# Down projections of three dense feed forwards split into single passes, with one rounding moved ahead of DMA issues

## The reference

```python
mod = cond @ w_ada[layer] + b_ada[layer]                 # 6 x 1024 numbers per layer
def swiglu(x, w1, w3, w2): return (silu(x @ w1) * (x @ w3)) @ w2          # first0
def conv_ffn(h, w_up, conv_w, conv_b, w_down):                            # even, odd
    gate, val = split(h @ w_up)
    gate = causal_dwconv(gate, conv_w) + conv_b          # 3 taps along the tokens
    return (silu(gate) * val) @ w_down
```

## Time and profile before

| | us |
|---|---|
| median of 3 runs | 2593.45 (2589.7 to 2593.66) |
| the profiled execution, its own time | 2587.25 |
| its span | 2585.4 |
| PE busy | 2504.0 |
| DVE busy | 1773.6 |
| ACT busy | 1199.2 |
| POOL busy | 333.2 |

### The profile page before, as it was taken

How to read it: one execution, slowest core, us unless ns; L and a number is a source line. 1 busy time by engine, 2 the same in 40 slices (tenths; PEclk the granted TensorE clock), 3 DMA queues, 4 the chain that set the end, 5 groups by cost and what they waited for, 6 DMA issues and landing times.

```text
span 2585.4 us, 36960 instructions
## 1 busy us (share of the span) xinstructions
PE 2504.0 (97%) x14304; PEld 2173.7 (84%) x14304; DVE 1773.6 (69%) x1949; ACT 1199.2 (46%) x1273; POOL 333.2 (13%) x97
## 2 busy tenths in 40 slices
PE   5999999999999999999999999899999999999999
PEld 4889998878888888888888888788999889988998
DVE  5832775768888888888888888365289777863122
ACT  3213213117676767676767676322322446653221
POOL 0005541000000000000000000010454100001542
PEclk8989999999999999999999999999999999999999
DMA  9745884767989998999999989230678443332442
GB/s 367 308 162 211 345 321 171 293 244 266 351 333 350 334 348 335 347 335 346 336 346 337 345 338 361 82 130 1 222 310 320 170 144 144 131 131 103 175 168 92
DMA packets 90383, 656.18 MB, mean 254 GB/s; under 512 B 10032, under 2 KB 10288, under 8 KB 10800
## 3 DMA queue, kind: packets, MB, share of 16 engines
q1 hardware_dynamic: 80928, 589.34, 60.8%
q10 hardware_dynamic: 9360, 65.52, 6.3%
HBM read 653.76 MB, written 1.05 MB: 253 GB/s over the span
## 4 chain that ended last, share of the span: by engine, by line
PE 71%; issue 17%; POOL 6%; DVE 3%; ACT 2%; ACTq 0%; DMA 0%; POOLq 0%; DVEq 0%; SPq 0%
PE bank L1158 70%; POOL ring_rounded L732 6%; PE bank L1703 1%; DVE work L1856 1%; DVE rstd L1904 0%; ACT ff_mid L1060 0%; DVE xT L1850 0%; DMA ring<-stream_dram 0%; DVE ring L1856 0%; DVE ring_rounded L1844 0%; ACT ff_silu L1059 0%; ACT work_rounded L773 0%; DVE yT L1850 0%; ACTq L753 0%; POOL work L692 0%
## 5 line engine op out<-in xcount | busy, mean ns | idle before, releaser
L1844 DVE TENSOR_TENSOR ring_rounded<-ring,work_rounded 128x2048 fp32r<-128x2048 f32 x372 | 842.1, 2289 | 143.6 <-ACT work_rounded L907 122.0
L1158 PE MATMUL bank<-work_rounded,proj_rounded 128*128 128x512 f32 x1792 | 614.3, 406 | 0.7 <-DVE proj_rounded L1844 0.3
L907 ACT ACTIVATE work_rounded<-ring 128x2048 fp32r<-128x2048 f32 x224 | 428.4, 1913 | 0.0
L1158 PEld LDWEIGHTS bank<-work_rounded,proj_rounded 128*128 128x128 f32 x1792 | 338.1, 189 | 77.1 <-issue 2.9
L1158 PE MATMUL bank<-ring_rounded,proj_rounded 128*128 128x512 f32 x896 | 354.1, 395 | 0.0
L1158 PE MATMUL bank<-work_rounded,ff_hid_rounded 128*128 128x512 f32 x896 | 302.5, 398 | 1.8 <-DVE ff_hid_rounded L1844 1.8
L1158 PE MATMUL bank<-yT_rounded,ring_rounded 128*128 128x256 f32 x960 | 271.6, 283 | 0.0
L1158 PE MATMUL bank<-hT,ring 128*128 128x256 f32 x1088 | 247.4, 388 | 1.1 <-ACT hT L797 1.1
L1158 PEld LDWEIGHTS bank<-hT,ring 128*128 128x128 f32 x1088 | 211.0, 195 | 37.8 <-issue 8.5
L1158 PE MATMUL bank<-ff_hid,ring 128*128 128x256 f32 x1056 | 232.9, 379 | 0.0
L1158 PEld LDWEIGHTS bank<-ff_hid,ring 128*128 128x128 f32 x1056 | 198.4, 190 | 25.9
(11 more groups left out here) (286 smaller groups left out, 4294.9 us busy)
## 6 DMA issues: line engine op xcount, KB each, us to landing
ring<-stream_dram SPq DMA_DIRECT2D x561, 1024.0 KB, 4.8
work<-stream_dram ACTq DMA_DIRECT2D x56, 1024.0 KB, 9.3
params<-params_dram ACTq DMA_DIRECT2D x1, 1728.5 KB, 28.8
consts<-consts_dram ACTq DMA_DIRECT2D x1, 1568.0 KB, 37.4
cond<-cond_dram ACTq DMA_DIRECT2D x2, 512.0 KB, 4.0
xT<-x_dram ACTq DMA_DIRECT2D x1, 1024.0 KB, 10.3
out_dram<-xT SPq DMA_DIRECT2D x1, 1024.0 KB, 3.9
consts<-consts_dram ACTq DMA_DIRECT2D x1, 577.0 KB, 32.2
```

Source lines behind the costliest of these rows:

```text
L907: act.activation(up_high[u][half], ring[:, (moe_first + s + half) % RING, :], ACT.Copy)\
L1158: return pe.matmul(o, lhsT=a, rhs=b, start=start, stop=stop, skip_group_check=True)
L1844: return dve.tensor_tensor(o, a, b, op)
```

## The change

The down slots of chunks 0 to 9 are made into single passes as the up slots are; the down of chunk 10 stays a float32 product. ACT rounds the down slot (`high(c, odd, 2)`) after `high(c, odd, 1)`, and before it the two hidden tiles of the chunk in one 128 x 512 instruction into `ff_hid_high` (`hid_high`); DVE subtracts that to get `ff_hid_low` (`leave_low`, `hid_low`), after the first two of the six dots where there are dots; POOL subtracts a third slot per chunk. `down(c)` waits on `split_low` and `hid_low` and does 48 float32r matmuls. ACT does `high(c, odd, 0)` ahead of `load_modulation`. Two more buffers of a slot lie in `work`, the tiles in `h_heads`; `cond` moves in memory.

```diff
+        ff_down_high = [work_r[:, mod_at + (MOD_GROUP + u) * SLOT:mod_at + (MOD_GROUP + 1 + u) * SLOT] for u in range(2)]
...
-        SPLITS = 2 * (DENSE_CHUNKS - 1)
-        PAIR_SPLITS = 4
+        SPLITS = 3 * (DENSE_CHUNKS - 1)
+        HID_SPLITS = DENSE_CHUNKS - 1
+        PAIR_SPLITS = 6
+        split_buffers = [w_high[0], w_high[1], ff_down_high[0], w_high[2], w_high[3], ff_down_high[1]]
...
+                    pool.wait_ge(weights_used, place[f"in{n}"])
+                    pool.wait_ge(split_low, dense_before[n] * SPLITS)
...
-                    at = (first + r // 2 * 3 + r % 2) % RING
+                    at = (first + r) % RING
                     pool.wait_ge(split_high, q + (before + 1))
-                    pool.tensor_tensor(ring_r[:, at, :], ring[:, at, :], f32(w_high[r]), ALU.subtract)\
+                    pool.tensor_tensor(ring_r[:, at, :], ring[:, at, :], f32(high), ALU.subtract)\
...
+                    if not final:
+                        high(c, odd, 0)
                     if n + 1 < len(plan) and not isinstance(c, int):
                         load_modulation(n + 1, c - 2)
-                    if not final:
-                        high(c, odd, 0)
                     if isinstance(c, int) and c == 0:
                         high(c, odd, 1)
                     tiles(c, odd)
                     if not (isinstance(c, int) and c == 0) and not final:
                         high(c, odd, 1)
+                    if not final:
+                        act.wait_ge(ffn_hid, base + 2 * c + 2)
+                        if not isinstance(c, int) or c >= 2:
+                            act.wait_ge(weights_used, c * 3 + (first - 1))
+                        act.activation(ff_hid_high[:, 2 * odd:2 * odd + 2, :], ff_hid[:, 2 * odd:2 * odd + 2, :], ACT.Copy)\
+                           .then_inc(hid_high, 1)
+                        high(c, odd, 2)
...
+                    else:
+                        r = 3 * c + 2
+                        q = splits + r + 1
+                        pe.wait_ge(split_low, q if i is None else i * PAIR_SPLITS + q)
+                        parts = [p.rearrange("p (j n) -> p j n", j=2)
+                                 for p in (ff_down_high[c % 2], ring_r[:, (first + 2 + r) % RING, :])]
+                        t = dense_before[n] * HID_SPLITS + c + 1
+                        pe.wait_ge(hid_low, t if i is None else i * 2 + t)
...
+                                last = mm3(o, [p[:, j, d * P:d * P + P] for p in parts],
+                                           (ff_hid_high[:, b, :], ff_hid_low[:, b, :]),
+                                           i is None and c == 0 and j == 0 and d % 2 == 0, False)
...
+                    def leave_low():
+                        dve.wait_ge(hid_high, c + (dense_before[n] * HID_SPLITS + 1))
+                        tt(ff_hid_low[:, 2 * odd:2 * odd + 2, :], ff_hid[:, 2 * odd:2 * odd + 2, :],
+                           f32(ff_hid_high[:, 2 * odd:2 * odd + 2, :]), ALU.subtract).then_inc(hid_low, 1)
+
...
+                            dve.wait_ge(hid_low, c + (dense_before[n] * HID_SPLITS - 1))
...
-                        mod_parts(n + 1, c - 2, range(MOD_GROUP))
+                        mod_parts(n + 1, c - 2, range(1))
+                        leave_low()
+                        mod_parts(n + 1, c - 2, range(1, MOD_GROUP))
+                    elif not (isinstance(c, int) and c == DENSE_CHUNKS - 1):
+                        leave_low()
```

More of the change, by code:

```diff
@@ L200, in build_program @@
         work = sb("work", shapes["work"])
-        cond = sb("cond", [P, D])
         ring_r, yT_r, ff_hid_r, work_r = (rounded[name] for name in ("ring", "yT", "ff_hid", "work"))
@@ L206, in build_program @@
         h_heads = sb("h_heads", shapes["h_heads"])
+        cond = sb("cond", [P, D])
         xT = sb("xT", [P, KD, T])
@@ L366, in build_program @@
         h_low = pflat_r[:, SLOT:2 * SLOT].rearrange("p (k t) -> p k t", k=KD)
-        assert mod_at >= 2 * SLOT
+        ff_down_high = [work_r[:, mod_at + (MOD_GROUP + u) * SLOT:mod_at + (MOD_GROUP + 1 + u) * SLOT] for u in range(2)]
+        assert mod_at >= 2 * SLOT and mod_at + (MOD_GROUP + 2) * SLOT <= work_n - D
+        ff_hid_high, ff_hid_low = (rounded["h_heads"][:, a * 4 * T:(a + 1) * 4 * T].rearrange("p (b t) -> p b t", b=4)
+                                   for a in range(2))
         weights_here = [sem(f"weights_here{i}") for i in range(RING)]
@@ L393, in build_program @@
         split_low = sem("split_low")
+        hid_high, hid_low = sem("hid_high"), sem("hid_low")
         ffn_mid = sem("ffn_mid")
@@ L726, in feed_forward, with low @@
                     .then_inc(*low_pool.step("h"))
-                def low(r, q):
-                    at = (first + r // 2 * 3 + r % 2) % RING
+                def low(r, q, high):
+                    at = (first + r) % RING
                     pool.wait_ge(split_high, q + (before + 1))
-                    pool.tensor_tensor(ring_r[:, at, :], ring[:, at, :], f32(w_high[r]), ALU.subtract)\
+                    pool.tensor_tensor(ring_r[:, at, :], ring[:, at, :], f32(high), ALU.subtract)\
                         .then_inc(split_low, 1)
@@ L736, in feed_forward @@
                     for r in range(PAIR_SPLITS):
-                        low(r, i * PAIR_SPLITS + r)
+                        low(r, i * PAIR_SPLITS + r, split_buffers[r])
             for n, kind in enumerate(plan):
@@ L1094, in high @@
                         act.wait_ge(weights_used, c * 3 + (first + w - 3))
-                    act.activation(w_high[2 * odd + w], ring[:, (first + at) % RING, :], ACT.Copy)\
+                    act.activation(split_buffers[3 * odd + w], ring[:, (first + at) % RING, :], ACT.Copy)\
                        .then_inc(split_high, 1)
@@ L1750, in split_here @@
                 def split_here(c, w, i):
-                    q = splits + 2 * (c - 1) + w + 1
+                    r = 3 * (c - 1) + w
+                    q = splits + r + 1
                     pe.wait_ge(split_low, q if i is None else i * PAIR_SPLITS + q)
-                    return w_high[2 * ((c - 1) % 2) + w], ring_r[:, (first + 3 * c - 1 + w) % RING, :]
+                    return split_buffers[r % PAIR_SPLITS], ring_r[:, (first + 2 + r) % RING, :]
                 def mm3(o, w, x, start, stop):
@@ L1790, in down @@
                 def down(c, i=None, final=False):
[L1791 to L1795, removed]
+                    if final:
+                        at = ff_down(first, c, chunks)
+                        arrive(at)
+                        pe.wait_ge(ffn_hid, base + 2 * c + 2)
+                    else:
+                        r = 3 * c + 2
+                        q = splits + r + 1
+                        pe.wait_ge(split_low, q if i is None else i * PAIR_SPLITS + q)
[3 more added lines that the diff above has]
+                        pe.wait_ge(hid_low, t if i is None else i * 2 + t)
                     for j in range(2):
@@ L1798, in down @@
                         for d in range(KD):
-                            last = mm(bank(d // 2, d % 2 * T, d % 2 * T + T), w2[:, j, d * P:d * P + P],
-                                      ff_hid[:, b, :], i is None and c == 0 and j == 0 and d % 2 == 0,
-                                      final and j == 1)
+                            o = bank(d // 2, d % 2 * T, d % 2 * T + T)
+                            if final:
+                                last = mm(o, down_k(at)[:, j, d * P:d * P + P], ff_hid[:, b, :], False, j == 1)
+                            else:
+                                last = mm3(o, [p[:, j, d * P:d * P + P] for p in parts],
+                                           (ff_hid_high[:, b, :], ff_hid_low[:, b, :]),
+                                           i is None and c == 0 and j == 0 and d % 2 == 0, False)
                             if final and j == 1 and d in (1, 3, 5):
```

## The result

The changed kernel takes 2654.83 us (median of 4 runs, 2653.57 to 2656.31) against 2591.57 of the kernel before in the same comparison (median of 4, 2582.69 to 2593.66). The ratio is 1.0256, with a 95% interval of [1.0244, 1.0269]. The profiled execution took 2654.68 us, 1.8 more than its span.

What follows compares the result with a forecast made beforehand. In `first0` and `even` a ring of ACT, DVE and POOL was taken to bound, in `odd` PE. `first0` +38.7, `even` +49.0 and `odd` -9.6 gave +78.1, on the median 2593.45 a forecast of 2671 us, range 2615 to 2690.

Steps and rivals of the forecast that it cites:

- The exclusion of DVE and POOL: In chunks with dots: while POOL subtracts no dot proceeds, exactly one does between two subtractions; chance of this mechanism 74%.
- Rivals 1: Rival 1: third subtraction costs nothing, intervals stay near 19.5 us, kernel faster at 2582, or 2565 with head overlapped; chance 5%.
- Rival 2: No head, as POOL does next chunk's w = 0 in it; 21.2 us bounds, +23.5 in all, 2617; chance 11%.
- Head: Stretch from a chunk's last dot to POOL's start, the shared resource idle: in `first0` 3.73 us before, 4.26 after, +0.53.
- +1.6: Growth of the head in `even`, where the convolution stands in it too; taken between +1.4 and +2.2 us.
- Moving the rounding buys nothing: ACT's new order: w = 0 leaves the head but w = 1 stands behind issues and SiLUs, so no gain.
- Third subtraction: POOL's added subtraction takes 4.55 us of the shared resource in each chunk; bounds 4.55 and 0.
- Hidden tiles: DVE's 128 x 512 subtraction adds 0.65 us to each chunk's ring, or 0 if it shared nothing with POOL.
- Intervals of 25.3 and 26.3: Predicted us between modulation issues per chunk in `first0` and `even`, +5.7 and +6.8, six intervals each.
- The tail: From group 7's issue to the last matmul, 33.0 us before: 28.7 in `first0` (-4.3), 32.4 in `even` (-0.6).
- the down in `odd`: Single passes take 5.76 us instead of 6.72, 0.96 less on PE for each of 10 chunks: -9.6.
- rival 3: PE's clock falls throughout, so its 17.3 us per chunk becomes 34.6 and bounds: 2790; chance 5%.

Runs made afterwards that it cites:

- all_dve: The changed kernel with all three subtractions of a chunk on DVE in place of POOL: 2548.18 us, ratio 0.9845 to the kernel before.
- order_only: The kernel before with only ACT's new order (first slot's rounding ahead of the modulation issues), no single-pass downs: 2602.08 us, ratio 1.006 to the kernel before.
- issue_first: The changed kernel with ACT's old order, modulation issues ahead of the rounding of w = 0: 2647.22 us, ratio 1.0232 to the kernel before.
- low_first: The changed kernel with DVE's 128 x 512 subtraction ahead of all six dots instead of after two: 2661.26 us, ratio 1.0293 to the kernel before.

## Why the prediction was right

**What bounds.** The exclusion of DVE and POOL held in every kernel in which POOL subtracts. With POOL out, no dot of the feed forwards takes longer than 1.15 us (all_dve); with all three subtractions on it, all three alternate with DVE's work. The chain of waits read over 264 to 410 us of the changed kernel has no PE in it, and 30% for the landing of the modulation group. That landing isn't the bound: it falls under POOL's first subtraction, and all_dve has the same transfers at 17.43 us a chunk.

**Rivals 1 and 2** fell. The third subtraction isn't free: POOL's idle time ahead of a set is 9.40 us, as it was the earlier trace rows, and is dots and head. Rival 2, the head of 4.26 gone and the interval 21.2, didn't come: no run with three subtractions on POOL is under 24.5.

**Head.** Predicted 4.26, measured 4.26, and 4.27 in order_only. In `even` +1.6 was a choice between 1.4 and 2.2: POOL starts 5.28 us after the last dot (2034.20 to 2039.48), +1.55, and order_only's interval there is +1.46. "Moving the rounding buys nothing" was right: it costs, as the two terms say, 13.7 us by itself, and issue_first gets 6 of it back.

**Third subtraction, +4.55.** POOL's three take 15.64 us, against 10.09 for two: 4.55 and one more gap of 1.0, in which a dot lies that had stood behind the set.

**Hidden tiles, +0.65.** 350.72 to 355.61 on DVE is one POOL subtraction waited out and 0.5 to 0.6 of its own; alone it takes 0.6. The Trainium skill (SBUF — State Buffer, Who interferes with whom) gives the rule that makes this a term, and the trace agrees: 4.97 us beside POOL, 0.68 with POOL silent. No run leaves this subtraction out alone, so its size is read from the one chunk.

**Sizes.** Intervals of 25.3 and 26.3 were 25.09 and 25.91. The hidden tiles account for most of the difference in `first0`: they add 0.47 us after POOL's last (355.14 to 355.61), for 0.65. In `even` the head has its 1.55, and from POOL's start to the last dot's end it is 20.60 us (2039.48 to 2060.08) against 15.77 before (1950.02 to 1965.79), +4.83 for +5.2: one dot slipped in ahead of POOL's first subtraction. Six intervals are +33.1 and +38.3 for +34.2 and +40.8. From the stage's start to group 1's issue it is +8.3 in both (259.95 - 252.03 in `first0`, whose start is 0.4 earlier) for +8.8. The tail is -4.3 in `first0`, as predicted, and -1.5 in `even` for -0.6. `first0` +37.2 for +38.7, `even` +45.2 for +49.0, and `odd` -12.4 for -9.6: +70.0 for +78.1, and the span grew by 67.5. The medians are 63.3 apart, and the rest of the way from 2671 to 2654.83 is the base: the median of before, on which the sum was put, was 6.2 us over the execution from which it was worked out. Put on that execution the sum gave 2665. So every term had its sign and the mechanism its place, while the total lies 0.2 us under the 2655 to 2685 that the prediction gave its own mechanism.

**The term that was off by the largest share** is the down in `odd`: -0.96 predicted, -1.24 measured (`ff_hid` comes every 18.43 us before and every 17.19 after, over nine chunks). A chunk of before was put at 18.2 where it takes 18.43. PE's timeline of the kernel before goes on behind the earlier trace rows with
```profile
2462.77 0.28 PE L1158 MATMUL bank<-proj_rounded,work_rounded 128*128 128x256 f32 x1
2462.89 0.28 PE L1158 MATMUL bank<-yT_rounded,ring_rounded 128*128 128x256 f32 x1
```
so the first rounded matmul behind a float32 down stands 0.31 us ahead of the next one, where 0.12 is the pitch: 0.19 that belongs to the down, and went with it. The pitch, 17.19/144 = 0.1194, makes 0.03 more, and 0.06 stay open. Ten chunks: -12.4 for -9.6. POOL in `odd` "just holds": PE has no wait for it there, and POOL is busy for 133.10 of 160 us.

**The clock.** In `first0` six chunks have an idle piece of 4.2 to 5.5 us ahead of the down, and PE went on at 0.50 after each. The Trainium skill (TensorE: Matmul & The Clock Gate, What's actually happening), which the prediction cites beside rival 3, has the throttled state as the default; the trace agrees here. Rival 3 itself, a fall throughout, didn't come. Its smaller form did, a fall of some 3 us within the spare time: PE idles 5.1 us in a chunk of `first0` (27.7 of 136, over 5.4 chunks) and not 8. The spare time covers it: in `first0` and `even`, from group 1's issue to the update of `xT`, no instruction of ACT or DVE waits for PE. In low_first that cover was perhaps not whole.

## What to carry to other kernels

Find out what sets the pace of a stage from the distance of a repeated event, and not from PE's busy share: here PE was 99% busy in `first0` and yet not the bound, with 18.43 us of work in a chunk of 19.58. Where, as here, DVE instructions with two SBUF operands meet POOL instructions that read SBUF, add the times of both as if they were one engine; then work that is twice as fast on DVE belongs on DVE, and a change that lost 2.6% gains 1.5% with that one move. Read the gain of an edit from the length of the stage: intervals inside it mislead, since its start and its tail move too.

## What was unexpected of the hardware

After idle pieces of 4.2 to 5.5 us ahead of a down PE went on at 0.50 each time, though it had been busy at 1.00 for 4 us and more until then; in `first0` the same followed one piece of 2.3 us (266.77 to 269.10). The window of 1624 to 1636 us in the earlier trace rows, a third idle in pieces of 1.2 to 2.2 us, showed no fall. And the order in which DVE and POOL get their turns is not fixed: in `even` a dot began 0.07 us ahead of POOL's first subtraction, kept its 1.15 us, and the subtraction took 5.54 us instead of 4.51.
